# Hybrid decoder layer: sums of the FFN product formed during gate/up, and loads of the down projection in rings

## The reference, cut to what matters

```python
h2 = rmsnorm(x, norm2)
x = x + (jax.nn.silu(h2 @ w_ffn_gate) * (h2 @ w_ffn_up)) @ w_ffn_down
```

## Time and profile before

| quantity | value |
|---|---|
| median of the runs shown | 1965.0 us |
| the profiled execution | 1963.27 us, span 1961.8 us |
| TensorE matmul busy | 1830.4 us (93%), 8612 matmuls |
| VectorE busy | 1147.7 us (59%) |
| ScalarE busy | 724.3 us (37%) |
| GpSimd busy | 579.6 us (30%) |
| mean granted TensorE clock | 0.977 |
| gate/up in full pace | 1315 to 1697 us |
| down | 1716.6 to 1958.5 us |

### The profile page before, as it was taken

How to read it: one execution, slowest core, us unless ns; L and a number is a source line. 1 busy time by engine, 2 the same in 40 slices (tenths; PEclk the granted TensorE clock), 3 DMA queues, 4 the chain that set the end, 5 groups by cost and what they waited for, 6 DMA issues and landing times. The chain is left out here.

```text
span 1961.8 us, 26601 instructions
## 1 busy us (share of the span) xinstructions
PE 1830.4 (93%) x8612; PEld 1513.4 (77%) x8612; DVE 1147.7 (59%) x1947; ACT 724.3 (37%) x1438; POOL 579.6 (30%) x662
## 2 busy tenths in 40 slices
PE   5999999999999799999989999769999999969998
PEld 4888878788787688888767888658888888757776
DVE  6542752743745748484856544674555545447987
ACT  5343342332334235353543222543332333224442
POOL 2211321311215325251511000224444434232543
PEclk9999999999999899999999999879999999989999
DMA  5112222122112111111136322312222212374344
GB/s 146 44 57 63 65 70 60 60 69 83 48 54 77 44 33 54 33 53 27 35 109 216 97 66 73 129 49 76 90 86 75 96 64 91 123 273 147 119 157 157
DMA packets 145390, 170.07 MB, mean 87 GB/s; under 512 B 8113, under 2 KB 104657, under 8 KB 144801
## 3 DMA queue, kind: packets, MB, share of 16 engines
q1 hardware_dynamic: 132768, 132.99, 21.5%
q0 software_dynamic: 7936, 27.77, 4.3%
q10 hardware_dynamic: 4608, 8.39, 1.1%
HBM read 135.41 MB, written 33.70 MB: 86 GB/s over the span
## 5 line engine op out<-in xcount | busy, mean ns | idle before, releaser
L1981 PE MATMUL bank<-act_hi,w_hi 128*128 128x512 f32 x1088 | 437.4, 402 | 2.5 <-DVE act_lo L1716 2.2
L1983 PE MATMUL bank<-act_hi,w_lo 128*128 128x512 f32 x1088 | 425.8, 391 | 0.0
L1982 PE MATMUL bank<-act_lo,w_hi 128*128 128x512 f32 x1088 | 424.9, 391 | 0.0
L1981 PEld LDWEIGHTS bank<-act_hi,w_hi 128*128 128x128 f32 x1088 | 205.3, 189 | 45.4 <-DVE act_lo L1716 3.3
L1983 PEld LDWEIGHTS bank<-act_hi,w_lo 128*128 128x128 f32 x1088 | 204.9, 188 | 44.2
L1982 PEld LDWEIGHTS bank<-act_lo,w_hi 128*128 128x128 f32 x1088 | 205.5, 189 | 39.9
L1981 PE MATMUL bank<-ca,wq_hi 128*128 128x512 f32 x528 | 208.8, 395 | 26.1 <-ACT p1b L1310 16.9
L1982 PE MATMUL bank<-ca,wq_hi 128*128 128x512 f32 x528 | 208.2, 394 | 0.0
L1983 PE MATMUL bank<-ca,wq_lo 128*128 128x512 f32 x528 | 207.9, 394 | 0.0
L1398 DVE TENSOR_TENSOR w_lo<-w_raw,w_hi 128x1024 fp32r<-128x1024 f32 x84 | 103.8, 1240 | 74.4 <-ACT w_hi L915 74.2
L1981 PEld LDWEIGHTS bank<-ca,wq_hi 128*128 128x128 f32 x528 | 100.8, 191 | 48.6 <-ACT p1b L1310 17.4
(11 more groups left out here) (312 smaller groups left out, 3614.9 us busy)
## 6 DMA issues: line engine op xcount, KB each, us to landing
w_raw<-in_w_in SPq DMA_DIRECT2D x60, 512.0 KB, 3.8
rawd<-in_w_ffn_down SPq DMA_DIRECT2D x99, 256.0 KB, 3.3
wr<-in_w_ffn_gate SPq DMA_DIRECT2D x11, 1024.0 KB, 5.5
wr<-in_w_ffn_up SPq DMA_DIRECT2D x11, 1024.0 KB, 5.4
y_scratch<-yq SPq DMA_DIRECT2D x44, 256.0 KB, 2.3
ya<-y_scratch SPq DMA_DIRECT2D x3, 2816.0 KB, 16.8
gate_scratch<-gbuf ACTq DMA_DIRECT2D x32, 256.0 KB, 2.1
gl<-gate_scratch POOLq DMA_DIRECT2D x16, 512.0 KB, 4.6
```

The lines of the kernel that those rows point to most:

```text
L1981: pe.matmul(ps, lhs_hi, rhs_hi, start=first, stop=False, skip_group_check=onto)
L1982: pe.matmul(ps, lhs_hi, rhs_lo, start=False, stop=False, skip_group_check=onto)
L1983: return pe.matmul(ps, lhs_lo, rhs_hi, start=False, stop=last, skip_group_check=onto)
```

## The change

Features are paired by even and odd tile in place of first and second half, so one iteration of gate/up yields all four quadrants of one step of down. Four sums (in the order of the products q = 2 to 5) are made by GpSimd in the iteration after (`y_sums`) into the new tile `sq`, and stored by one transfer of 1 MB; quadrants 0, 1 and 3 of the four blocks are stored alone, and the scratch tensor holds seven operands of 256 KB for each of the 11 steps. In down `ya4` and `sx` are gone: step n loads its operand into the ring `rx` (8 slots) and its one or two weight tiles into `rawd`. x2 has its own tile `xq`, loaded after steps 8, 14, 20 and 26. The adds of x2 on GpSimd are done earlier, and the results are stored in three transfers of 1 MB and four of 256 KB. On VectorE `d_lo(0)`, `d_lo(1)` each come one product later in the last pair, and `d_lo(2)` comes after the last addition to `yq`.

```diff
+    op_d = nc.dram_tensor("y_scratch", (FK, 7, P, HALF), F32).ap()
+        sq = sb("sq", [P, 4, HALF])
-        ya4 = sb("ya4", [P, 4, FK, HALF])
+        rx = sb("rx", [P, 8, HALF])
+        xq = sb("xq", [P, 4, 4, HALF])
-        sx = sb("sx", [P, FK, HALF])
...
+        def store_sums(i):
+            sp.wait_ge(sum_pool, SP0 + 4 * i + 4)
+            alone(sp)
+            sp.dma_start(op_d[bass.ds(i, 1), 2:6].rearrange("a j p t -> p (a j) t"), sq[:, :, :]).then_inc(sq_out, 16)
...
             if not first:
-                sp.wait_ge(ym_done, 3 * i)
-                store_y(i - 1, 3)
+                store_sums(i - 1)
...
+        def load_step(n):
+            q, kt = n // FK, n % FK
+            r = raw_at[(q, kt)] + len(RAWS[q]) - 1 - 8
+            if n >= 8:
+                sp.wait_ge(wlo_done, W0 + 2 * (n - 8) + 1)
+            if r >= 0:
+                last_use = max(FK * a + b for (a, b), at in raw_at.items() if at <= r)
+                sp.wait_ge(wlo_done, W0 + 2 * last_use + 2)
+            if kt == FK - 1:
+                sp.wait_ge(y_out[{0: 0, 1: 1, 6: 2}[q]] if q in (0, 1, 6) else sq_out, 16 * NF_IT)
+            sp.dma_start(rx[:, n % 8, :], op_d[kt, q]).then_inc(rd_in[n % 8], 16)
+            for k, part in enumerate(RAWS[q]):
...
+                rows = P * (2 * kt + kh)
+                sp.dma_start(rawd[:, (raw_at[(q, kt)] + k) % 8, :],
+                             w_fd[rows:rows + P, HALF * dh:HALF * dh + HALF]).then_inc(rd_in[n % 8], 16)
...
+        for n in range(4):
+            load_step(n)
         ffn_store(ND)
+        for n in range(4, 8):
+            load_step(n)
+        store_sums(ND)
         sp.wait_ge(prod, done(NPAIR - 1, 6))
+        for n in range(8, NSTEP):
+            load_step(n)
+            if n in (8, 14, 20, 26):
+                load_x2((n - 8) // 6)
...
+        def y_sums(i):
+            pool.wait_ge(ym_done, 3 * i + 3)
+            pool.wait_ge(y_done, Y0 + i + 1)
+            pool.wait_ge(sq_out, 16 * i)
+            a11, a12, a22, a21 = (yq[:, k, :] for k in range(4))
+            pool.tensor_tensor(sq[:, 0, :], a21, a22, ALU.add).then_inc(sum_pool, 1)
+            pool.tensor_tensor(sq[:, 3, :], a11, a21, ALU.subtract).then_inc(sum_pool, 1)
+            pool.wait_ge(sum_pool, SP0 + 4 * i + 1)
+            pool.tensor_tensor(sq[:, 1, :], sq[:, 0, :], a11, ALU.subtract).then_inc(sum_pool, 1)
+            pool.wait_ge(sum_pool, SP0 + 4 * i + 3)
+            pool.tensor_tensor(sq[:, 2, :], a12, sq[:, 1, :], ALU.subtract).then_inc(sum_pool, 1)
+
         def ffn_pool(i, first=False, last=False):
             if not first:
                 y_mult(i - 1, 3)
             t_adds(2 * i + 1, 1, i)
+            if not first:
+                y_sums(i - 1)
...
+        pool.wait_ge(d_evac, 4)
+        store_out(0, pd[:, 1, :, :])
+        pool.wait_ge(dx_in[3], 16)
         for m in range(4):
+            pool.wait_ge(d_evac, 4 + m + 1)
+            x2_add(2, 3, m)
+        pool.wait_ge(dx_in[1], 16)
         for m in range(4):
+            pool.wait_ge(d_evac, 8 + m + 1)
+            x2_add(1, 1, m)
+        pool.wait_ge(dx_in[2], 16)
         for m in range(4):
+            x2_add(0, 2, m)
```

More of the change, by code:

```diff
@@ L85, in decoder_layer @@
     x2_t = x2_d.rearrange("(tt p) d -> p tt d", p=P)
-    y_d = nc.dram_tensor("y_scratch", (2 * FK, P, S), F32).ap()
+    op_d = nc.dram_tensor("y_scratch", (FK, 7, P, HALF), F32).ap()
     ctx = ExitStack()
@@ L234, in decoder_layer @@
         ps = sb("ps", [P, 2, 2, HALF])
+        sq = sb("sq", [P, 4, HALF])
     with ExitStack() as mem:
         sb = on(mem)
-        ya4 = sb("ya4", [P, 4, FK, HALF])
+        rx = sb("rx", [P, 8, HALF])
+        rawd = sb("rawd", [P, 8, HALF])
+        xq = sb("xq", [P, 4, 4, HALF])
         pd = sb("pd", [P, 3, 4, HALF])
-        rawd = sb("rawd", [P, 8, HALF])
-        sb("at_wq", [P, 2 * 8 * HALF])
-        sx = sb("sx", [P, FK, HALF])
         tx = sb("tx", [P, FK, HALF])
@@ L304, in decoder_layer @@
     p1_done, evac, gs_done, ym_done = sem("p1_done"), sem("evac"), sem("gs_done"), sem("ym_done")
-    y_out = [sem(f"y_out{i}") for i in range(4)]
-    ya_in = [sem(f"ya_in{i}") for i in range(5)]
+    y_out = [sem(f"y_out{i}") for i in range(3)]
+    sq_out = sem("sq_out")
     rd_in = [sem(f"rd_in{i}") for i in range(8)]
     dprod, d_evac, out_pool = sem("dprod"), sem("d_evac"), sem("out_pool")
-    dx_in = [sem("dx_in0"), sem("dx_in1")]
+    dx_in = [sem(f"dx_in{i}") for i in range(4)]
     F0 = 2 * NK
@@ L396, in decoder_layer @@
             raw_at[(q_, kt_)] = sum(FK * len(RAWS[k]) for k in range(q_)) + kt_ * len(RAWS[q_])
+    step_in = [16 * sum(1 + len(RAWS[m // FK]) for m in range(n % 8, n + 1, 8)) for n in range(NSTEP)]
     XS, YS = (0, 1, 2, 6), (3, 4, 5, 7)
@@ L484, in store_y @@
         def store_y(i, k):
-            f, xh = (0, 1, 1, 0)[k], (0, 0, 1, 1)[k]
             alone(sp)
-            sp.dma_start(y_d[bass.ds(2 * i + f, 1)].rearrange("a p t -> (a p) t")[:, HALF * xh:HALF * xh + HALF],
+            sp.dma_start(op_d[bass.ds(i, 1), (0, 1, 6)[k]].rearrange("a p t -> (a p) t"),
                          yq[:, k, :]).then_inc(y_out[k], 16)
+        def store_sums(i):
+            sp.wait_ge(sum_pool, SP0 + 4 * i + 4)
+            alone(sp)
+            sp.dma_start(op_d[bass.ds(i, 1), 2:6].rearrange("a j p t -> p (a j) t"), sq[:, :, :]).then_inc(sq_out, 16)
         for tt in range(6):
@@ L525, in _ @@
         ffn_io(NF_IT - 1, last=True)
[L527 to L532, removed]
-                kh, dh = part // 2, part % 2
[L534 to L547, removed]
+        def load_step(n):
[10 more added lines that the diff above has]
+            for k, part in enumerate(RAWS[q]):
+                kh, dh = part // 2, part % 2
+                rows = P * (2 * kt + kh)
+                sp.dma_start(rawd[:, (raw_at[(q, kt)] + k) % 8, :],
+                             w_fd[rows:rows + P, HALF * dh:HALF * dh + HALF]).then_inc(rd_in[n % 8], 16)
@@ L549, in _, with load_x2 @@
+        def load_x2(part):
+            th, dh = part // 2, part % 2
+            sp.dma_start(xq[:, part, :, :], x2_t[:, 4 * th:4 * th + 4, HALF * dh:HALF * dh + HALF]
+                         ).then_inc(dx_in[part], 16)
         ND = NF_IT - 1
-        sp.wait_ge(wlo_done, wn(NPAIR - 2, 6))
-        for kt in range(4):
-            load_raw(0, kt)
         sp.wait_ge(prod, done(NPAIR - 1, 1))
-        for k in (0, 1, 2, 3):
+        for k in range(3):
             sp.wait_ge(y_out[k], 16 * ND)
-        for s_, (k0, k1) in enumerate(((0, 1), (1, 4), (4, FK))):
-            load_y(0, k0, k1, s_)
+        sp.wait_ge(sq_out, 16 * ND)
@@ L558, in _ @@
+        for n in range(4):
+            load_step(n)
         ffn_store(ND)
[L559 to L563, removed]
-        sp.wait_ge(prod, done(NPAIR - 1, 6))
[L565 to L590, removed]
+        for n in range(4, 8):
+            load_step(n)
@@ L594, in _ @@
         sp.wait_ge(out_done, 16 * 4)
-        sp.wait_ge(out_pool, 16 * 9)
+        sp.wait_ge(out_pool, 16 * 3)
     @block.gpsimd
@@ L862, in _ @@
         y_mult(NF_IT - 1, 3)
[L864 to L889, removed]
@@ L890, in _, with store_out, x2_add @@
-        pool.wait_ge(dx_in[0], 32)
+        y_sums(NF_IT - 1)
+        def store_out(part, t):
+            th, dh = part // 2, part % 2
+            pool.dma_start(out_t[:, 4 * th:4 * th + 4, HALF * dh:HALF * dh + HALF], t).then_inc(out_pool, 16)
+        def x2_add(k, part, m):
+            pool.tensor_tensor(pd[:, k, m, :], pd[:, k, m, :], xq[:, part, m, :], ALU.add).then_inc(ym_done, 1)
+        pool.wait_ge(d_evac, 4)
+        store_out(0, pd[:, 1, :, :])
+        pool.wait_ge(dx_in[3], 16)
@@ L891, in _ @@
         for m in range(4):
[L892 to L895, removed]
+            pool.wait_ge(d_evac, 4 + m + 1)
+            x2_add(2, 3, m)
+        pool.wait_ge(dx_in[1], 16)
         for m in range(4):
-            pool.tensor_tensor(pd[:, 0, m, :], pd[:, 0, m, :], ya4[:, 0, m, :], ALU.add).then_inc(ym_done, 1)
+            pool.wait_ge(d_evac, 8 + m + 1)
+            x2_add(1, 1, m)
@@ L910, in _ @@
+        pool.wait_ge(d_evac, 16)
+        store_out(1, pd[:, 1, :, :])
+        pool.wait_ge(d_evac, 20)
+        store_out(3, pd[:, 2, :, :])
     @block.scalar
@@ L1350, in d_hi @@
                 act.wait_ge(prod, ST0 + n - 3)
[L1351 to L1361, removed]
+            act.wait_ge(rd_in[n % 8], step_in[n])
+            act.copy(wq_hi[:, n % 4, :], rx[:, n % 8, :]).then_inc(whi_done, 1)
             r = raw_at[(q, kt)]
             if q in (0, 1, 4):
-                act.wait_ge(rd_in[r % 8], 16 * (r // 8 + 1))
                 src = rawd[:, r % 8, :]
@@ L1842, in room @@
                         dve.wait_ge(y_out[k], 16 * i)
+                        dve.wait_ge(sum_pool, SP0 + 4 * i)
             dve.wait_ge(prod, done(p, 0))
@@ L1854, in pair_dve @@
                     if not first:
```

(30 more changed lines are left out.)

## The result

The changed kernel takes 1932.07 us (median of 4 runs, 1931.7 to 1932.66) against 1964.42 us (4 runs): a ratio of 0.9835, 95% interval 0.9818 to 0.9852. That is 32.4 us, where 1932.3 us and 32.7 us were forecast. In a second set of runs it took 1932.76 against 1963.81 us, 0.9845 (0.9829 to 0.9862).

What follows compares the result with a forecast made beforehand. Gate/up was taken as full on TensorE, with 32.2 us lost in down and 6.7 ahead of it. Gains of 27.3 and 5.4 us, together 32.7, gave 1932.3 us; likeliest case 1928 to 1938, 8-in-10 range 1927 to 1943.

Steps and rivals of the forecast that it cites:

- Start of down: Between product 5's last matmul and down: earlier operand load and moved low parts gain 5.4 us, bounds 0 to 6.
- Stall at step 8 and its clock: Step 8 of down: without the block of y loads, 16.2 us idle and 1.5 us at lower clock go.
- The sums out of down: Down without GpSimd's 44 adds: of 12.1 us of slow pace, waits and clock, 1.2 stay for x2 adds.
- Three loads a step: q = 2 and q = 5 of down: passages with 1 MB transfers beside the tiles cost 0.8 us, bounds 0 to 15.
- signs of being wrong: Longer gate/up iterations, waits for `rd_in` in q = 2 or q = 5, or a landing over 7 us there.
- The rival of small loads that don't overlap: q = 2 and q = 5: three tiles land one after another, 145 us lost, 2077 us in all; chance 0.01.
- Gate/up: The new sums fit into GpSimd's idle time in gate/up: 0 us, between 0 and 1.9 us an iteration.
- Product 6 ends at 1711.2, the addition to `yq` at 1711.9: Start of down: addition right behind product 6, then `y_mult` at 1713.6 and the last four sums at 1720.3 us.
- an issue by 1726 is in time. 6 us are left: Step 8 loads, queued behind the last sums' store: with landing of 3.1 to 4.7 us, 6 us of cover.
- worst, the sums cost twice as much and 1 or 2 us come back: Worst case at step 8 of down: slower last sums take back 1 or 2 of the 17.7 us gained.
- The rival of the moved wait: SyncE waits for the last iteration's sums, or idle before product 6 lowers the clock: 5 to 10 us back, 1940; chance 0.07.

Runs made afterwards that it cites:

- kernel of the early low parts: Changed kernel with `d_lo(0)` to `d_lo(2)` one product earlier each in VectorE's order: 1934.25 us.
- kernel with cut loads: Kernel before, y quadrants 1 to 3 loaded in nine parts between the weight tiles of steps 8 to 17, x2 after step 18: 1947.5 us, ratio 0.9919.
- thin sums: Kernel before, GpSimd's 44 sums in down made on 16 columns of 512, quadrant 0 as operand in their place: 1957.98 us, ratio 0.9969.
- twice the sums: Changed kernel with four more 128 x 512 additions in each set of sums inside gate/up, not in the last: 1932.75 us.
- late sums: Changed kernel with four more additions before the sums of the last iteration only: 1940.84 us; with x2 loads also moved later, 1940.89 us.
- the kernel before with the two counts: Kernel before, waits for product 6 of the last pair and ScalarE's wait before high parts each lowered by one count: 1958.69 us, ratio 0.9965.

## Why the prediction was right, and where its steps were off

**Start of down** (5.4 forecast, 5.45 measured). Right in place and cause: operand 0 first, line 1851 (1888 before) no longer late, an idle of 0.96 us that left the clock at its upper level. The kernel of the early low parts shows that moving them wasn't needed for this.

**Stall at step 8 and its clock** (17.7). Gone. The kernel with cut loads gained 17.8 us between the first matmul of down and step 11.

**The sums out of down** (10.9: 12.1 less 1.2). The thin sums shortened q = 2, q = 3 and q = 5 by 5.7 us, and once the stall was gone by 8.5 with the last product; the rest is the x2 adds. They cost 0.73 and 0.38 us at 1810 and 1846, with restarts 1.3: 1.2 was taken.

**Three loads a step** (0.8). 0.5 us in q = 2 and nothing in q = 5. The size was right, though it varies (0 to 1.5 us in the other profiles). Two of the prediction's own signs of being wrong did appear: ScalarE and VectorE waited for tiles in q = 2 and q = 5, and tiles issued from 1768 to 1798 us landed after 3.4 to 8.9 us, where "over 7 us" was the sign. Both were signs too early in the chain: the ring of eight slots kept all but 0.16 us of it from TensorE. The rival of small loads that don't overlap is out: three tiles a step landed with a median of 5.1 us, and the step took 2.8.

**Gate/up** (0). Right; twice the sums are free too.

**Two steps failed.** The first is "Product 6 ends at 1711.2, the addition to `yq` at 1711.9", with nothing in the sum for what stands beside it. The addition waits for step 0 of down too and comes at 1713.06. Behind it the low parts of steps 2 to 4 run beside GpSimd's last sums at 3.39 us a step, and VectorE has no lead. They are late by 0.5 us each, 2.0 with the slower pace behind each restart. Three runs bear this out: with the addition on time, or with the low parts a product earlier, the waits at steps 2 to 4 are gone; with four adds more there are two waits more. This is most of the 2.4 us by which down fell short (24.9 for 27.3). The text ahead of it had ScalarE's wait wrong too (step n - 4; it is n - 3), so VectorE's lead over TensorE was a step shorter than taken. That the total came out within 0.3 us owes something to chance: in the profile the gain is 31.4 us, 1.3 short of the forecast, and 1.0 of it lies ahead of down, where profiles of one kernel differ by more.

The second is "an issue by 1726 is in time. 6 us are left", and "worst, the sums cost twice as much and 1 or 2 us come back". The sums were stored at 1722.37 and not at 1720.3, and the landing was taken from a quiet stretch, 3.1 to 4.7 us; behind the released burst it is

```profile
DMA to landing us min/median/max: 5.7/8.7/9.9
```

(weight tiles issued from 1722 to 1734 us). In the changed kernel the low parts of step 8 are ready at 1731.1 us, 2.8 ahead of its first matmul, and those of step 9 1.5 ahead. Less than half of the 6 us was there, and 6.8 us of delay cost 7.1. The rival of the moved wait was the closest one, and its price of 5 to 10 us was right.

## What to carry to other kernels

Read the order of an in-order DMA queue against what is needed first: a tile wanted at once, written behind megabytes that are wanted later, cost 17.8 us here, more than any arithmetic. Don't add up causes from separate experiments: a stall can cover another cost, which comes out once it is gone (the sums: 5.7 us with the stall, 8.5 without). When cover is counted in microseconds, take the landing time of the stretch in which the transfer will run, with the burst that its own release sets off. And when a wait ends later than the work it names, count the semaphore by hand: two counts, each one too high, cost 3.9 us here, and the waits they made looked like contention alone.

## What the runs showed of the hardware

The clock after an idle of TensorE. Behind idles of 4.00 us (product 6 before) and 3.72 and 3.69 us (step 8 with late sums) the matmuls went on 0.43 us apart, the lower level of 1.2 GHz; behind one of 3.68 us (product 6 with cut loads) they went on at 0.23, the upper level of 2.4 GHz. Ahead of the idles of 4.00 and 3.68 us TensorE had been busy without a gap; ahead of that of 3.72 it had had five short ones. Shorter idles went both ways as well: behind 2.09 us (before) and 2.03 us (cut loads) the clock fell within a few matmuls, and behind 2.08 us (cut loads) and 2.12 us (the kernel before with the two counts) it stayed up. So in these profiles the length of the idle alone doesn't tell what the clock does.

VectorE beside GpSimd. Its additions that read PSUM kept 0.68 to 0.69 us in gate/up with GpSimd busy 163 us of 382, 220 and 282 alike. Its operations with both inputs in SBUF took 0.68 us alone and up to 1.8 beside GpSimd's adds, in gate/up as in down; one took 4.72 us, from 1797.78 us in the kernel before.

The same load of 256 KB took from 2.7 to 12.7 us from issue to landing, depending on what was in flight: 2.7 to 4.7 with two tiles a step (before), 3.4 to 8.9 with three loads a step, 5.7 to 9.9 in the burst behind the last sums, and 10.0 to 12.7 behind the block of y loads.
